# Inverting a triangular matrix's 16 x 16 blocks by forward substitution on VectorE instead of by matmuls

## What is computed

```python
a_low = jnp.where(strict, jnp.einsum('bhncd,bhnjd->bhncj', kb, kc) * decay_mat, 0.0)
eye = jnp.eye(CHUNK, dtype=jnp.float32)
rhs = jnp.concatenate([vb, kb * jnp.exp(gcum)[..., None]], axis=-1)
sol = lax.linalg.triangular_solve(eye + a_low, rhs, left_side=True, lower=True, unit_diagonal=True)
u, w = sol[..., :GDN_V_DIM], sol[..., GDN_V_DIM:]
```

## Time and profile before

| what | value |
|---|---|
| median of three runs | 526.4 us |
| profiled execution, its own time | 529.0 us |
| its span | 527.1 us |
| mean granted TensorE clock | 0.966 |
| PE busy / weight load / DVE / ACT / POOL | 477.2 / 366.0 / 195.0 / 124.7 / 15.3 us |
| DMA | 135.88 MB, mean 258 GB/s |

### The profile page before, as it was taken

How to read it: one execution, slowest core, us unless ns; L and a number is a source line. 1 busy time by engine, 2 the same in 40 slices (tenths; PEclk the granted TensorE clock), 3 DMA queues, 4 the chain that set the end, 5 groups by cost and what they waited for, 6 DMA issues and landing times.

```text
span 527.1 us, 10734 instructions
## 1 busy us (share of the span) xinstructions
PE 477.2 (91%) x4533; PEld 366.0 (69%) x4533; DVE 195.0 (37%) x531; ACT 124.7 (24%) x309; POOL 15.3 (3%) x47
## 2 busy tenths in 40 slices
PE   5999999999999999999999999999978676788664
PEld 4885889897699878998855567677665554656341
DVE  2055126963121434562221254443424232323123
ACT  3000132201101132332002443333322231222125
POOL 8011000000000000000000000000000000000000
PEclk9999999999999999999999889999979899889888
DMA  8547487434124040404469839999999999999942
GB/s 302 133 162 281 161 357 282 153 123 160 55 106 158 3 149 12 160 1 159 160 250 423 331 129 421 421 373 409 424 418 421 423 421 421 422 418 420 420 183 85
DMA packets 32941, 135.88 MB, mean 258 GB/s; under 512 B 5312, under 2 KB 5632, under 8 KB 20608
## 3 DMA queue, kind: packets, MB, share of 16 engines
q1 hardware_dynamic: 28992, 134.26, 64.5%
q10 hardware_dynamic: 3760, 0.47, 0.6%
q0 software_dynamic: 144, 0.52, 0.3%
HBM read 134.20 MB, written 1.05 MB: 257 GB/s over the span
## 4 chain that ended last, share of the span: by engine, by line
PE 71%; DMA 19%; DVE 6%; issue 1%; ACT 1%; SPq 1%; DVEq 0%; ACTq 0%
PE ps L764 26%; DMA ring<-in_moe_w_up 18%; PE ps L1090 7%; PE ps L1059 6%; PE ps L997 5%; PE ps L982 5%; PE ps L781 5%; PE ps L1111 3%; PE ps L1121 2%; PE ps L774 2%; PE ps L1099 1%; PE ps L1039 1%; DVE arena L1282 1%; DVE arena L1369 1%; PE ps L932 1%
## 5 line engine op out<-in xcount | busy, mean ns | idle before, releaser
L764 PE MATMUL ps<-arena 128*128 128x256 f32 (+1 forms) x640 | 163.3, 408 | 1.4 <-DVE arena L1260 1.4
L764 PEld LDWEIGHTS ps<-arena 128*128 128x128 f32 x640 | 120.2, 193 | 30.2 <-issue 14.7
L1090 PE MATMUL ps<-ring,arena 128*32 128x128 f32 x1408 | 56.0, 304 | 30.3 <-DMA ring<-in_moe_w_up 30.3
L1090 PEld LDWEIGHTS ps<-ring,arena 128*32 128x32 f32 x1408 | 43.0, 119 | 42.7 <-DMA ring<-in_moe_w_up 32.9
L602 ACT ACTIVATE arena<-ps 32x256 f32<-32x256 f32 x64 | 24.2, 378 | 57.9 <-PE ps L1111 57.5
L1059 PEld LDWEIGHTS ps<-arena 128*128 128x128 f32 x256 | 30.5, 199 | 2.5 <-issue 2.3
L1121 PE MATMUL ps<-arena,rw 128*128 128x512 f32 x64 | 31.1, 631 | 1.1 <-DVE arena L1686 1.1
L1059 PE MATMUL ps<-arena 128*128 128x128 f32 x256 | 32.0, 285 | 0.0
L1686 DVE COPY arena<-ps 32x256 f32<-32x256 f32 x64 | 26.7, 417 | 12.6 <-PE ps L1111 11.5
L997 PE MATMUL ps<-arena 128*128 128x512 f32 x64 | 28.3, 595 | 0.0
L982 PE MATMUL ps<-arena 128*128 128x256 f32 x128 | 28.0, 379 | 0.0
(11 more groups left out here) (247 smaller groups left out, 463.6 us busy)
## 6 DMA issues: line engine op xcount, KB each, us to landing
ring<-in_moe_w_gate SPq DMA_DIRECT2D x22, 1024.0 KB, 16.8
ring<-in_moe_w_up SPq DMA_DIRECT2D x22, 1024.0 KB, 18.9
ring<-in_moe_w_down SPq DMA_DIRECT2D x22, 1024.0 KB, 16.3
arena<-in_w_in SPq DMA_DIRECT2D x9, 2048.0 KB, 8.2
arena<-in_moe_w_gate SPq DMA_DIRECT2D x10, 1024.0 KB, 15.0
arena<-in_moe_w_up SPq DMA_DIRECT2D x10, 1024.0 KB, 17.5
arena<-in_moe_w_down SPq DMA_DIRECT2D x10, 1024.0 KB, 15.9
arena<-in_w_out SPq DMA_DIRECT2D x2, 2048.0 KB, 8.3
```

What stands on the lines that cost most here:

```text
L764: last = pe.matmul(out, lhs, rhs, start=(k == 0), stop=(k == KD - 1))
L1090: last = pe.matmul(c.ps[ROWS * q:ROWS * (q + 1), i % 2, 0:P], c.Hg[par][:, k, ROWS * i:ROWS * (i + 1)], c.gu_w[slot][:, :, k, start:start ...
```

## The change

Only levels four and five (blocks of 16 to 32, and 32 to 64) are still made by products. The inverses of the 64 diagonal blocks of 16 x 16 (8 matrices x 8 blocks) are made on VectorE, one block to a partition, by 15 steps of forward substitution, two instructions each. To bring the blocks onto 64 partitions and back, ScalarE's queue stores A to DRAM (512 KB), loads the blocks from it (rows of 64 bytes), stores the inverse and its transpose to two other DRAM places (again rows of 64 bytes), which GpSimd's queue has filled with zeros, and loads both as `TT` and `T` (512 KB each). The projection parts that stood between the lower levels move: `dk` 3, `dv` 0 and half of `dv` 1 now stand ahead of Y4, and from there on every part comes earlier against the recurrence by two parts; one part, `ma0` 3, stands between "wT" and the scores. The blocks, their inverses and the products live in `Yb`.

The diff, cut (the list of semaphores, GpSimd's masks and the renamed counts are left out):

```diff
-LEVELS = 5
+
+BLOCK = 16
+BLOCKS = 2 * H * P // BLOCK
+LEVELS = (4, 5)
 SIDE = [("consts", 1), ("bd", 1), ("ss", 1), ("rnk", 1), ("rnq", 1), ("gsum", 1), ("grow", 1), ("gram", 1),
-        ("intra", 1), ("ktok", 1), ("vtok", 1), ("b1", 1)]
-for _l in range(1, LEVELS + 1):
-    SIDE += [(f"Y{_l}", 1), (f"TT{_l}", 1)] + ([(f"T{_l}", 1)] if _l < LEVELS else [])
+        ("intra", 1), ("ktok", 1), ("vtok", 1)]
+for _l in LEVELS:
+    SIDE += [(f"Y{_l}", 1), (f"TT{_l}", 1)] + ([(f"T{_l}", 1)] if _l < LEVELS[-1] else [])
...
+    for place in c.stored[1:]:
+        pool.dma_start(tiles_of(place), c.zeros.rearrange("p (a f) -> p a f", a=2 * H)).then_inc(s["blocks_zeroed"], 16)
...
+    act.wait_ge(s["A_ready"], 1)
+    act.dma_start(tiles_of(c.stored[0]), c.flat["A"].rearrange("p (a f) -> p a f", a=2 * H)).then_inc(s["A_stored"], 16)
+    act.wait_ge(s["A_stored"], 16)
+    act.dma_start(c.block, blocks_of(c.stored[0])).then_inc(s["blocks_loaded"], 16)
     evacuate("dk", c.flat["kT"], "dk_ready", ACT.Copy)
-    take_T(1)
+    act.wait_ge(s["blocks_inverted"], 2)
+    act.wait_ge(s["blocks_zeroed"], 32)
+    for place, blocks in zip(c.stored[1:], (c.inverseT, c.inverse)):
+        act.dma_start(blocks_of(place), blocks).then_inc(s["blocks_stored"], 16)
+    act.wait_ge(s["blocks_stored"], 32)
+    for place, name in zip(c.stored[1:], ("TT", "T")):
+        act.dma_start(c.flat[name].rearrange("p (a f) -> p a f", a=2 * H), tiles_of(place)).then_inc(s["inverse_loaded"], 16)
     evacuate("dv", c.flat["dv"], "dv_ready", ACT.Copy)
-    take_T(2)
-    take_T(3)
+    take_T(4)
     evacuate("ma0", c.mg[0], "mg_ready", ACT.Sigmoid)
-    take_T(4)
...
-    pe.wait_ge(s["b1_ready"], 1)
-    turn("b1", lambda i: c.Yb[:, i // 4, i % 4, :])
     project("dk", 2)
-
+    project("dk", 3)
+    project("dv", 0)
...
+        if lv == LEVELS[0]:
+            pe.wait_ge(s["inverse_loaded"], 32)
+        else:
+            pe.wait_ge(s["TT_ready"], 1)
             turn(f"T{lv - 1}", lambda i: c.TT[:, i // 4, i % 4, :])
         each(f"Y{lv}", lambda t, h: c.A[:, t, h, :], lambda t, h: c.TT[:, t, h, :])
 
...
-    level_y(1)
-    project("dk", 3, range(KD // 2))
-    level_t(1)
-    project("dk", 3, range(KD // 2, KD))
-    level_y(2)
-    project("dv", 0)
-    level_t(2)
-    project("dv", 1)
-    level_y(3)
+    project("dv", 1, range(KD // 2))
+    level_y(4)
+    project("dv", 1, range(KD // 2, KD))
+    level_t(4)
     project("ma0", 0)
-    level_t(3)
+    level_y(5)
     project("ma0", 1)
-    level_y(4)
+    level_t(5)
     project("ma0", 2)
-    level_t(4)
-    project("ma0", 3)
-    level_y(5)
-    project("ma1", 0)
-    level_t(5)
-    project("ma1", 1)
-    pe.wait_ge(s["TT_ready"], LEVELS + 1)
+    pe.wait_ge(s["TT_ready"], 2)
...
+    project("ma0", 3)
     scores(0)
-    project("ma1", 2)
+    project("ma1", 0)
     pe.wait_ge(s["wT_ready"], 1)
     state_out(0)
-    project("ma1", 3)
+    project("ma1", 1)
     turn_probs(0)
     state_in(1)
-    project("mb0", 0)
+    project("ma1", 2)
     weigh_values(0)
     state_out(1)
+    project("ma1", 3)
+    scores(1)
+    project("mb0", 0)
+    state_in(2)
     project("mb0", 1)
-    scores(1)
-    project("mb0", 2)
-    state_in(2)
-    project("mb0", 3)
     state_out(2)
     turn_probs(1)
-    project("mb1", 0)
+    project("mb0", 2)
     state_in(3)
     weigh_values(1)
+    project("mb0", 3)
+    state_out(3)
+    project("mb1", 0)
     project("mb1", 1)
-    state_out(3)
-    project("mb1", 2)
     pe.wait_ge(s["ya_ready"], 1)
     turn("yaT", lambda i: c.oa[:, i % 2, (i // 2) * P:(i // 2 + 1) * P])
+    project("mb1", 2)
     project("mb1", 3)
...
+def tiles_of(place):
+
+    return place.rearrange("(a r) -> a r", a=2 * H)[:, 0:P * P].rearrange("a (p f) -> p a f", p=P)
+
+
+def blocks_of(place):
+
+    return place.rearrange("(q r) -> q r", q=BLOCKS)[:, 0:BLOCK * P].rearrange("q (i f) -> q i f", i=BLOCK)[:, :, 0:BLOCK]
...
+    v.wait_ge(s[f"side_free{side_pair('gram')}"], side_reuse("gram") + 1)
+    settle()
+    v.sem_inc(s["A_ready"], 1)
+    chain(v.memset(c.inverse, 0.0))
 
     ps = side("intra")
     side_done("intra", v.tensor_tensor(c.flat["attnT"], c.flat["attnT"], ps, ALU.mult))
-
-    v.wait_ge(s[f"side_free{side_pair('gram')}"], side_reuse("gram") + 1)
     settle()
-    A8, Y8 = (c.flat[x].rearrange("p (a f) -> p a f", a=8) for x in ("A", "Yb"))
-    T8, TT8 = (c.flat[x].rearrange("p (a f) -> p a f", a=8) for x in ("T", "TT"))
+    chain(v.memset(c.inverse.rearrange("q i j -> q (i j)")[:, 0:BLOCK * BLOCK:BLOCK + 1], 1.0))
+    Y8 = c.flat["Yb"].rearrange("p (a f) -> p a f", a=8)
...
-    v.tensor_tensor(Y8, A8, all8(c.m1), ALU.mult).then_inc(s["b1_ready"], 1)
...
+    v.wait_ge(s["blocks_loaded"], 16)
+    for j in range(BLOCK - 1):
+        n_, w = BLOCK - 1 - j, j + 1
+        outer = c.outer[:, 0:n_ * w].rearrange("q (i j) -> q i j", i=n_)
+        under = c.inverse[:, w:BLOCK, 0:w]
+        chain(v.tensor_tensor(outer, c.block[:, w:BLOCK, j:j + 1].to_broadcast([BLOCKS, n_, w]),
+                              c.inverse[:, j:j + 1, 0:w].to_broadcast([BLOCKS, n_, w]), ALU.mult))
+        settle()
+        last = v.tensor_tensor(under, under, outer, ALU.subtract)
+        if w < BLOCK - 1:
+            chain(last)
+            settle()
+    last.then_inc(s["blocks_inverted"], 1)
+    v.wait_ge(s["blocks_inverted"], 1)
+    v.tensor_copy(c.inverseT, c.inverse.rearrange("q i j -> q j i")).then_inc(s["blocks_inverted"], 1)
...
-    v.wait_ge(s["b1_ready"], 1)
-    v.tensor_tensor(T8, all8(c.ident), Y8, ALU.subtract).then_inc(s["T_ready"], 1)
-    ps = side("b1")
-    last = v.tensor_tensor(TT8, all8(c.ident), ps.rearrange("p (a f) -> p a f", a=8), ALU.subtract)
-    last.then_inc(s["TT_ready"], 1)
-    v.wait_ge(s["TT_ready"], 1)
-    v.sem_inc(s[f"side_free{side_pair('b1')}"], 1)
-    for lv in range(1, LEVELS + 1):
+    for n_, lv in enumerate(LEVELS):
...
-        if lv == 1:
+        if n_ == 0:
```

More of the change, by code:

```diff
@@ L152, in lay_out @@
     c.S = v3(at("S", 512), H)
+    c.zeros = at("vn", 1024)
     c.vn = [v3(at("vn", 512, 512 * i), H) for i in range(2)]
@@ L157, in lay_out @@
     c.aT = at("Yb", 1024)
+    c.block, c.inverse, c.inverseT = (at("Yb", BLOCK * BLOCK, 256 * i)[0:BLOCKS].rearrange("q (i j) -> q i j", i=BLOCK) for i in range(3))
+    c.outer = at("Yb", 256, 768)[0:BLOCKS]
     c.yaT, c.ybT = v3(at("qT", 1024), H), v3(at("kT", 1024), H)
@@ L178, in lay_out @@
     m = sb("masks", [P, 14, P])
-    c.ident, c.ones, c.before, c.upper, c.lower, c.chunk, c.half0, c.half1, c.m1 = (m[:, i, :] for i in range(9))
-    c.levelT = [m[:, 9 + i, :] for i in range(LEVELS)]
+    c.ident, c.ones, c.before, c.upper, c.lower, c.chunk, c.half0, c.half1 = (m[:, i, :] for i in range(8))
+    c.levelT = [m[:, 9 + i, :] for i in range(max(LEVELS))]
     c.masks = m
@@ L237, in lay_out @@
         q_normed k_normed gsum_ready gsum_exp grow_pre grow_exp qdec_ready
-        tok_ready b1_ready Y_ready TT_ready T_ready wT_ready
+        tok_ready A_ready A_stored blocks_loaded blocks_zeroed blocks_inverted blocks_stored inverse_loaded Y_ready TT_ready T_ready wT_ready
         dq_ready dk_ready dv_ready mg_ready
@@ L363, in gpsimd_program @@
                        pattern=[[-1, P]], channel_multiplier=1).then_inc(s["ident_ready"], 1)
-    odd = c.m1.rearrange("p (a b) -> p a b", b=2)[:, :, 0]
-    settle(pool.affine_select(out=odd, in_=odd, compare_op=ALU.not_equal, fill=1.0, base=-1,
-                              pattern=[[-2, P // 2]], channel_multiplier=1))
     for v in (c.upper, c.lower, c.chunk, c.half0, c.half1, c.ones, c.before):
@@ L369, in gpsimd_program @@
     tops = []
-    for lv in range(LEVELS):
+    for lv in (level - 1 for level in LEVELS):
         w = 2 << lv
@@ L1840, in build @@
         c = lay_out(nc, ctx)
+        c.stored = [nc.dram_tensor(f"stored{i}", (2 * H * (P * P + P),), F32, kind="Internal").ap() for i in range(3)]
         block = ctx.enter_context(nc.Block())
```

15 lines of the change are left out of this document (7 added, 8 removed).

## The result

The changed kernel takes **518.9 us** (median of 4 runs, 515.66 to 521.70), the kernel before beside it 526.2 (4 runs, 524.98 to 526.49). The ratio is 0.986, with a 95% interval of 0.982 to 0.990: faster by 7.2 us, where 13.7 were forecast. The profiled execution took 518.0 (span 516.3, mean clock 0.965).

What follows compares the result with a forecast made beforehand. TensorE's matmuls were taken to bound the rewritten stretch: 14.2 us of work removed plus 0.3 of wait covered, less 0.8 waiting at Y4, gives 13.7; from the median 526.4 that forecasts 512.7 us, range 511.0 to 521.0.

Steps and rivals of the forecast that it cites:

- late inverse: Rival, 0.21: block stores and loads meet `ma0`'s weight load; TensorE waits 5 us at Y4, clock loss costs 3.5; 520.4 us.
- the third term of the sum: TensorE's wait for the inverse before Y4, from 128.9 to 129.7: 0.8 us taken off the gain.
- Link 1: A is ready at about 103.0; ScalarE is copying `dq`, so its store of A is issued at 103.5.
- link 3: Load of the blocks from DRAM, 1024 pieces of 64 bytes: 2.5 us taken between 2.3 and 8.2, done at 111.5.
- link 4: Substitution on VectorE, 30 dependent instructions: 7.2 us, plus 0.45 for the turned copy, done at 119.2.
- Link 2: Store of A to DRAM, 512 KB: 5.5 us, the middle between the output store's 2.7 and a w_in load's 8.2.
- Link 5: ScalarE copies `dk` first, so block stores are issued at 119.8, hiding up to some 0.6 us of earlier lateness.
- Link 6: Two stores of the inverted blocks, 2048 pieces of 64 bytes: 4.6 us taken between 3.6 and 8.2, done at 124.4.
- Link 7: Two loads of 512 KB, the inverse and its transpose: 5.2 us taken between 4.3 and 8.2, done at 129.6.
- the slower case: Rival, 0.10: 64-byte pieces crawl at 130 in a us, inverse lands about 149, TensorE waits 20 us; 535 us.
- Edits at nothing: Zero stores, later "vtok" scaling, moved E multiplication and qdec copy, held `dv` copy, later `mb0`: all covered, costing nothing.
- The tail: Last stretch, expert loads: starts at TensorE's word, so savings survive; rival, 0.05, has it take them back, 526.4 us.

Runs made afterwards that it cites:

- `dv` held longer: Against the changed kernel, SP issues the load of the `dv` weights only when the blocks of A are loaded; 518.5 us, ratio 0.985 to the kernel before.

## Why the range held and the forecast wait did not

The forecast's time, 512.7, was missed by 6.2 us; the stated range, 511.0 to 521.0, holds the 518.9 only because it was drawn wide enough for the rival "late inverse", to which I gave 0.21 and which came. What failed is the third term of the sum, the wait of 0.8 us with the clock kept: it is 5.4, and 2.0 for the clock. The chain in us behind "ktok":

| | forecast | measured |
|---|---|---|
| store of A issued | 0.6 | 0.7 |
| A stored | 6.1 | 9.0 |
| blocks loaded | 8.6 | 11.8 |
| inverted and turned | 16.3 | 19.2 |
| dk copied (gate) | 16.9 | 16.8 |
| blocks stored | 21.5 | 25.7 |
| inverse loaded | 26.7 | 31.5 |
| TensorE at Y4 | 26.0 | 26.1 |
| wait | 0.8 | 5.4 |

- **The work removed** was right: 14.22 us measured for 14.2. The scores' wait of 0.3 went too.
- **Link 1** (issue), **link 3** (2.8 us for 2.5) and **link 4** (7.3 for 7.65) were right. The widths from the routing's instructions carried over well.
- **Link 2 failed.** I took the middle between a lone store and a shared load, 5.5; it was the upper end, 8.3. This was the first failure and brought 2.9 us of lateness (9.0 for 6.1), of which the gate's slack of 0.6 swallowed a part: 2.3 us of it reached the stores of the blocks.
- **Link 5** was wrong only through link 2: the copy of `dk` gated nothing, since the chain came 2.4 us behind it. The run with `dv` held longer shows the gate as I described it.
- **Link 6 failed**, in size: 6.5 us with its issue for 4.6. I had named the load of `ma0` as its upper end and then taken one us over the lower. **Link 7** took 5.8 for 5.2. Links 2, 6 and 7 with 2.3, 1.9 and 0.6 us make up the 4.8 by which the inverse landed late.
- **The upper end was added up wrongly.** Links 2, 3, 6 and 7 at 8.2 each give 103.5 + 16.4 + 7.65 + 16.4 = 144 and a wait of 15, not 139 and 10. By the prediction's own sums that end is the slower case, past the 140 from which the change loses. No run here came near it.
- **The rival's argument** was right in kind: the block stores meet `ma0`'s load, TensorE waits, the clock falls. Its landing (31.1 behind "ktok" for 31.5 measured) was luck in part: its own terms, 119.8 + 8.2 + 7, give 135.0, which is 32.1, it had all the lateness in links 6 and 7 (15.2 us for 12.3 measured), and none in link 2, where it began. What I held against it, that `ma0`'s load is over by 126.8, was true and no help: the stores are issued at 118.86, 3.4 us behind that load (115.46), and none of their packets runs before 122, when it is nearly through (rows below). Its clock term was too high, 3.5 for 2.0. I had read 8 us of low clock in a stretch where TensorE stood idle in part, and here the next stretch is back at 0.97 within 4 us.
- **Edits at nothing** cost nothing: without the transfers TensorE has no new wait from "ktok" to the routing, and the zeros (5.6 us, issued at 49.83) delay nobody.
- **The tail** passes the gain on, as argued. "Slower" is excluded as a mechanism: 64-byte pieces alone run at 1000 and more in a us, not 130, and the inverse lands 31.5 us behind "ktok", where this rival needed about 46.
- **The pages.** The fixed part of 2.0 us and the penalty on small writes were held against links 6 and 7. The 2.0 (the Trainium skill, "DMA: Bandwidth & Descriptors", Anatomy of one DMA) is given there for transfers that GpSimd issues; these are ScalarE's. Issued at 115.51, both block stores have landed at 118.78 in the run with nothing beside them, 3.3 us for the two with the issues in it; the forecast's lower end was 3.6. The Trainium skill, "DMA: Bandwidth & Descriptors", Specifications, has pieces under 512 B read, modified and written; the doubling was my guess from it, and no run shows one.

The account of the change: 14.5 removed, 5.4 of wait and 2.0 of clock added, 7.1 gained; 526.2 - 7.1 = 519.1, measured 518.9. The runs' scatter (515.7 to 521.7) is wider than that agreement.

## What to carry to other kernels

A transfer on a chain has two prices, alone and beside whatever load is in flight, and here they differed by a factor of 2 to 3. List what each leg runs beside, and take the upper end wherever a large load was issued within the last microseconds. Holding back one load moves the collision to the next leg; it paid here only when all loads stood clear of the chain, or when the chain overtook the gate that coupled it to the load. And where TensorE's clock fell in a wait, that cost 1.5 to 2.9 us on top of its length, while behind waits of 1.32 and 2.10 us it had not fallen; so a little more cover ahead of a wait can be worth more than its own length.
